# A hybrid decoder step in four groups: group barriers and the loop replaced by one straight program with semaphores that count on

## What is computed

```
xn = rms_norm(h, norm_mix)
qa, ka, va, qkv_b, z, a, b, gate_logits = split(xn @ w_in)
oa = sliding-window attention with sinks (qa, ka, va)
qb, kb, vb = silu(short_conv(qkv_b));  ob = gated delta rule(qb, kb, vb, a, b), gated norm with z
ga, gb = split(sigmoid(gate_logits))
h = h + (ga * (oa @ w_oa) + gb * (ob @ w_ob)) @ w_out
hn = rms_norm(h, norm_ffn)
h = h + (silu(hn @ w_gate) * (hn @ w_up)) @ w_down
y = rms_norm(h, norm_final)
```

## Time and profile before

| | us |
|---|---|
| median of 3 runs | 3794.16 (3791.37 to 3797.62) |
| the profiled execution | 3792.9 |
| its span, first to last instruction | 3791.1 |
| TensorE busy | 3594.3 (95%) |
| VectorE busy | 1808.2 (48%) |
| ScalarE busy | 1330.6 (35%) |
| GpSimd busy | 307.4 (8%) |

### The profile page before, as it was taken

One profiled execution on the slowest core, in us unless ns is written; L12 is line 12 of the kernel. 1 busy time (PEld: TensorE's weight loads), 2 busy tenths in 40 slices (PEclk: granted clock), 3 DMA queues, 4 the chain that ended last, 5 costly groups with the idle time before them and its releaser, 6 DMA issues. The chain is left out here.

```text
span 3791.1 us, 49730 instructions
## 1 busy us (share of the span) xinstructions
PE 3594.3 (95%) x20199; PEld 3103.6 (82%) x20199; DVE 1808.2 (48%) x3160; ACT 1330.6 (35%) x2360; POOL 307.4 (8%) x297
## 2 busy tenths in 40 slices
PE   6879999999998999999998999999998999999997
PEld 6768888999997888788877888788886888788886
DVE  3844332543434744454344744454344654455344
ACT  3532333322223544432223544432223543442222
POOL 2111110000001211000000311000000221100000
PEclk9978889999999999999999999999999999999998
DMA  4101001322232211233333211233323211133323
GB/s 161 45 30 41 29 28 43 111 84 84 84 133 89 72 35 34 73 113 99 95 128 110 73 34 34 67 111 100 95 99 122 89 40 34 59 109 100 95 95 131
DMA packets 89484, 303.98 MB, mean 80 GB/s; under 512 B 12384, under 2 KB 14384, under 8 KB 88336
## 3 DMA queue, kind: packets, MB, share of 16 engines
q1 hardware_dynamic: 89248, 300.68, 24.3%
HBM read 289.04 MB, written 12.62 MB: 80 GB/s over the span
## 5 line engine op out<-in xcount | busy, mean ns | idle before, releaser
L611 PE MATMUL bank<-hnT,wh 128*128 128x512 f32 (+1 forms) x3520 | 931.4, 352 | 0.0
L1519 DVE TENSOR_TENSOR wl<-raw,wh 128x1024 fp32r<-128x1024 f32 (+1 forms) x472 | 585.6, 1241 | 651.0 <-ACT wh L1161 648.7
L611 PE MATMUL bank<-xnT,wh 128*128 128x512 f32 (+2 forms) x2560 | 746.4, 378 | 12.4 <-DVE d_dT L1753 9.7
L611 PEld LDWEIGHTS bank<-hnT,wh 128*128 128x128 f32 x3520 | 619.4, 188 | 91.4 <-issue 0.2
L1161 ACT CAST wh<-raw 128x1024 fp32r<-128x1024 f32 (+1 forms) x472 | 492.3, 1043 | 435.7 <-PE bank L611 329.4
L611 PE MATMUL bank<-hnT,wl 128*128 128x512 f32 (+1 forms) x1760 | 622.2, 354 | 0.0
L611 PEld LDWEIGHTS bank<-xnT,wh 128*128 128x128 f32 x2560 | 454.5, 196 | 81.3 <-DVE d_dT L1753 11.0
L611 PE MATMUL bank<-hid,wh 128*128 128x512 f32 (+1 forms) x1760 | 468.6, 354 | 6.4 <-DVE wl L1519 5.1
L611 PE MATMUL bank<-xnT,wl 128*128 128x512 f32 (+2 forms) x1280 | 471.0, 368 | 0.0
L611 PEld LDWEIGHTS bank<-hnT,wl 128*128 128x128 f32 x1760 | 330.6, 188 | 45.8
L611 PEld LDWEIGHTS bank<-hid,wh 128*128 128x128 f32 x1760 | 309.3, 188 | 55.1 <-DVE wl L1519 8.1
(11 more groups left out here) (300 smaller groups left out, 4647.1 us busy)
## 6 DMA issues: line engine op xcount, KB each, us to landing
raw<-in_wstream SPq DMA_DIRECT2D x474, 512.0 KB, 3.4
xr<-in_x_prompt SPq DMA_DIRECT2D x20, 512.0 KB, 5.1
xT<-in_xT SPq DMA_DIRECT2D x5, 2048.0 KB, 11.9
hT<-in_xT SPq DMA_DIRECT2D x4, 2048.0 KB, 9.0
out_yp_out<-hT SPq DMA_DIRECT2D x16, 512.0 KB, 3.0
raw<-in_wstream SPq DMA_DIRECT2D x8, 528.0 KB, 3.4
Sb<-in_state_delta SPq DMA_DIRECT2D x1, 2048.0 KB, 12.4
out_ds_out<-Sb SPq DMA_DIRECT2D x1, 2048.0 KB, 6.4
```

The source lines that it names most:

```text
L611: ins = nc.tensor.matmul(*a, **k)
L1519: v_.tensor_tensor(wl[n % HL][:, 0:m], raw[:, n % RAW, 0:m], wh[n % HL][:, 0:m].bitcast(F32), ALU.subtract).then_inc(sem("lo_done"), 1)
```

## The change

All four groups are written out one after another, and each engine has one list from the prologue to the epilogue: one block in place of many, no barrier between groups, no loop, no clearing of semaphores.

- Since nothing sets a semaphore back, each wait that counts within a group now adds what earlier stages have counted: `made(name, v)` adds to v from a table COUNTS of what the prologue, group 0 and each later group add.
- The ring of weights runs on over the groups: unit numbers are g * NU + n. A group's last roundings on ACT and DVE already include the next group's first two units, by the same rule "two units ahead" that holds inside a group; `ahead_hi` and `ahead_lo` are gone.
- TensorE's claims on its eight banks go on over the join, and at each a1 unit it waits for two further chunks of the normed input.
- The scratch tokens' last norm stands in group 1, beside the last norm of group 0's prompt tokens (banks 5 and 6, semaphores with an S in their names). Their output is stored there.
- Group 3 no longer loads and norms a next group's input or rounds weights for it.
- ACT waits, ahead of the squares of each delta tile, for POOL's root of the tile before.

The diff, cut to its core (nearly every other line only moves to the left or wraps a wait in `made`):

```
+    now = [0]
+    def made(name, v):
+        pro, first, later = COUNTS.get(name, (0, 0, 0))
+        k = now[0]
+        return sem(name), v + (pro if k > 0 else 0) + (first if k > 1 else 0) + later * max(k - 2, 0)
...
-    def ahead_hi(act, n):
-        act.wait_ge(sem(f"ahead_in{n}"), 16)
-        act.copy(wh[n][:, 0:width(n)], raw[:, n, 0:width(n)]).then_inc(sem("ahead_hi"), 1)
-    def ahead_lo(dve, n):
-        dve.wait_ge(sem("ahead_hi"), n + 1)
...
+    def load_until(sp, n):
+        while asked[0] <= min(n, NG * NU - 1):
+            k = asked[0]
+            if k >= RAW:
+                sp.wait_ge(sem("lo_done"), k - RAW + 1)
+            m = width(k % NU)
+            sp.dma_start(raw[:, k % RAW, 0:m], d["wstream"][k % NU][:, 0:m]).then_inc(sem(f"raw_in{k % RAW}"), 16)
+            asked[0] += 1
...
             def unit(name, i):
-                    n = UNIT_AT[(name, i)]
-                    if n >= PRE:
-                        pe.wait_ge(sem("lo_done"), n - PRE + 1)
+                n = g * NU + UNIT_AT[(name, i)]
+                pe.wait_ge(sem("lo_done"), n + 1)
...
                         if u == 0:
                             claim(abank[t], "a_rd", q + 1)
+                        if q == 0:
+                            pe.wait_ge(*made("xl_done", 2 * u + 2 - KD))
...
                     if not first and u == 0:
                         claim(2, "ypre_done", 1)
+                        pe.wait_ge(*made("yacc_done", 0))
                         last_sums(pe, tiles, 2)
+                        if g == 1:
+                            claim(5, "ypreS_done", 1)
+                            last_sums(pe, ["S"], 5, "S")
...
-                if first:
-                    pe.wait_ge(sem("yacc_done"), KD - 1)
-                    claim(7, "ypre_done", 1)
-                    last_sums(pe, ["S"], 7)
-                    claim(4, "y_done", KD)
-                    last_spread(pe, ["S"], 4)
...
-                while split[0] <= min(UNIT_AT[(name, i)] + AHEAD, NU - 1):
+                while split[0] <= min(g * NU + UNIT_AT[(name, i)] + AHEAD, NG * NU - 1):
...
-                for n in range(PRE):
-                    dve.wait_ge(sem("unit_started"), NU - 1 + n)
-                    ahead_lo(dve, n)
...
-    prologue()
-    nc.all_engine_barrier(sems_to_clear=range(nums[0], nums[-1] + 1))
-    group(0, True)
-    nc.all_engine_barrier(sems_to_clear=range(nums[0], nums[-1] + 1))
-    with nc.Fori(1, NG) as g:
-        group(g, False)
-        nc.all_engine_barrier(sems_to_clear=range(nums[0], nums[-1] + 1))
-    epilogue()
+    stages = [prologue()] + [group(g, g == 0) for g in range(NG)] + [epilogue()]
+    with nc.Block() as block:
+        @block.tensor
+        def _(pe):
+            claim = make_claim(pe)
+            for stage in stages:
+                stage[1](pe, claim)
```

More of the change, by code:

```diff
@@ L336, in claim @@
                 pe.wait_ge(*released[b])
-            released[b] = (sem(s), v)
+            released[b] = made(s, v)
         return claim
-    def last_sums(pe, order, b):
-        row_sums(pe, order, b, acc, "ysum_ps")
-    def last_pre(dve, order, b):
-        n = n_of(order[0])
-        dve.wait_ge(sem("ysum_ps"), 1)
-        nc.vector.tensor_scalar(yr[0:n, 0:len(order)], bank[b][0:n, 0:len(order)], 1.0 / DM, EPS, ALU.mult,
-                                ALU.add).then_inc(sem("ypre_done"), 1)
@@ L358, in last_spread, with last_root @@
+    def last_root(pool, order, x=""):
+        n, q = n_of(order[0]), 0 if x == "" else NT
+        pool.wait_ge(*made(f"ypre{x}_done", 1))
+        nc.gpsimd.tensor_tensor(yr[0:n, q:q + len(order)], yr[0:n, q:q + len(order)], nhalf[0:n, 0:len(order)],
+                                ALU.pow).then_inc(sem(f"yrr{x}_done"), 1)
+    def last_spread(pe, order, b, x=""):
+        q0 = 0 if x == "" else NT
+        pe.wait_ge(*made(f"yrr{x}_done", 1))
         for q, t in enumerate(order):
-            last = spread(t, yr, q, bank[b][:, P * q:P * q + n_of(t)])
@@ new lines, in tensor, with scalar @@
+        def tensor(pe, claim):
+            now[0] = 0
+            pe.wait_ge(*made("ident_in", 16))
+            for q, t in enumerate(tiles):
+                pe.wait_ge(*made("rr_done", q + 1))
+                spread(t, rr, q, bank[5][:, 0:NS] if t == "S" else bank[6][:, P * t:P * (t + 1)]).then_inc(sem("xR_ps"), 1)
+            pe.wait_ge(*made("const_in", 16))
+        def scalar(act):
+            now[0] = 0
+            act.wait_ge(*made("param_in", 16))
+            act_steps[0] += 1
+            act.activation(nal[:], p("alog"), ACT.Exp).then_inc(sem("act_step"), 1)
+            for q, t in enumerate(tiles):
+                act.wait_ge(*made(f"x_in{t}", 32 if t == "S" else 16))
+                x_square(act, t, q, xr0[t])
+            for k in range(KD):
+                x_hi(act, k, xT0, every)
@@ new lines, in tensor, with scalar, gpsimd, vector @@
+        def tensor(pe, claim):
+            now[0] = 1 + NG
+            claim(2, "ypre_done", 1)
+            pe.wait_ge(*made("yacc_done", 0))
+            last_sums(pe, order, 2)
+            claim(7, "y_done", KD)
+            last_spread(pe, order, 7)
+        def scalar(act):
+            pass
+        def gpsimd(pool):
+            now[0] = 1 + NG
+            last_root(pool, order)
+        def vector(dve):
+            now[0] = 1 + NG
+            last_pre(dve, order, 2)
+            last_scale(dve, order, 7)
@@ L502, in group @@
+        return sync, tensor, scalar, gpsimd, vector
     def group(g, first):
@@ L1718, in _ @@
-                dve.wait_ge(sem("tail_done"), NCONV)
-                lo_until("conv", NCONV - 1)
-                quarters = [0]
-                def beside(t, k):
-                    for _ in range(0 if t == "S" else QUARTERS[k]):
-                        quarters[0] += 1
-                        if quarters[0] % 4 == 0:
-                            lo_until("gate", quarters[0] // 4 - 1)
-                    if after(t) is not None:
-                        attention_step(after(t), IN_DELTA_S if t == "S" else IN_DELTA, k)
```

2785 lines of the change are left out of this document (1431 added, 1354 removed).

## The result

The changed kernel takes 3724.01 us in the median of four runs (3722.45 to 3731.46), against 3792.76 (3789.59 to 3797.62) for the kernel before on the same chip. The ratio is 0.9822, with a 95% interval from 0.9804 to 0.9839. The forecast was 3735, with a range of its own from 3726 to 3746. The direction and the mechanism held. The kernel before was 1.4 us faster here than the 3794.16 that the forecast started from; 0.9822 of 3794.16 is 3726.6, at the range's edge. The profiled execution took 3722.45 us, 70.4 less in its span than the one before, where 58.7 had been worked out.

The account below looks back on a forecast made before the run. TensorE's work and its pauses were taken as the bound. Joins 46.2, start 2.6 and end 9.9 make 58.7 us off the profiled 3792.9: 3734.2, plus 1.3 for the median, forecast 3735; own range 3726 to 3746, given range to 3752.

Parts of the forecast that it names:

- What bounds the kernel: Whole kernel: TensorE, busy 3594.3 of 3791.1 us, plus the places where it stands still, the long ones at the joins.
- The joins: Three group joins, last matmul to first sum: 64.1 us become 17.2, less 0.7 for scratch tokens' steps; gain 46.2 us.
- All three covers: At the joins, TensorE's work hides VectorE's tail; thinnest, the first unit covers the `acc` sums by 0.3 us.
- the first rival: Joins close only in part, the first unit needing VectorE's tail: 16 to 22 us given back, 3751 to 3757; 12 in 100.
- The start: Group 0's start: TensorE waits for the first unit's low part alone, starting at about 30.05, not 32.69; gain 2.6 us.
- The end: Group 3's spreads and epilogue: 0.8 fewer spreads, 7.2 earlier sums, 1.9 full pace; gain 9.9 us, or 8.0 if pace fell.
- I take the full pace for both: Last sums and spreads in the epilogue: 0.95 and 1.05 us instead of 1.86 and 2.08; gain 1.9 us.
- Group 3: Group 3 prepares no next input, so TensorE loses 8 spreads; gain some 0.8 us.
- The delta stages: Delta stages: instructions and order unchanged; the granted clock may shift the time by 8 us either way.
- a sign of being wrong: Prediction wrong if the three joins give back over 10 us, or the delta stages change by more than that.
- The slower program on account of instruction fetches: Rival: the written-out program stalls on instructions; 42 stops of 3.6 us would cost 151 us, 3886; 2 in 100.
- the loop's head: Join at the loop's head: TensorE starts 3.6 us after SP, put down to the jump; already in the sum.

Follow-up runs that it names:

- The kernel with barriers: Changed kernel with each stage in its own block, a barrier of all engines between blocks and no loop: 3759.63 us, ratio 0.9916.
- the copy: The changed kernel run a second time, word for word: 3727.09 us, ratio 0.9829.
- The kernel with the loads alone: Changed kernel, but group 3 still loads a next input and does not norm it: 3730.08 us, ratio 0.9833.
- the one with the loads apart: Changed kernel with first two weight units rounded early, idle matmuls at start and end, and next-input loads spread between weights in SP's queue: 3710.86 us, ratio 0.9785.
- the kernel with early units: Changed kernel, but the prologue rounds the first two weight units after the second and fourth input chunk, not the eighth: 3720.75 us, ratio 0.9814.

## Why the prediction was right, and where it was off

**What bounds the kernel** held: TensorE's work and its pauses. Apart from the added matmuls, every difference that the traces could place was a pause of TensorE or went with its clock.

**The joins** came as forecast, 47.1 us for 46.2. All three covers held, the thinnest by 0.14 us. The kernel with barriers shows what would be left if only the loop had gone (35.6 us given back), and the one that waits for the whole input what the first rival would have cost: 20.3 us at the joins, inside the 16 to 22 that it was priced at, and 24.5 in all.

**The start** gave 2.2 for 2.6. VectorE's two low parts began later than the 28.78 of the earlier trace rows, and TensorE began 0.15 us behind the first of them, as forecast:

```profile
29.15 2.36 DVE L1615 TENSOR_TENSOR wl<-raw,wh 128x1024 fp32r<-128x1024 f32 x2 [0.20 <-ACT wh L1261]
```

The pause before it stayed, and 8 us of it could be had by casting earlier.

**The end** had one step that failed: "So I take the full pace for both: 1.9 us more." Only the sums had it in the profiled execution (1.02 us; the spreads 2.05), and in the copy neither had (1.84 and 2.05). The ground for the step was a pair of such matmuls at 0.32 us behind a pause of 5.24, and eight behind a shorter pause did not follow it every time. The term was 0.9 and can be 0. Without the 0.8 of group 3 the forecast for the end was 9.1, or 7.2 if the pace had fallen. Measured were 7.9, and 7.1 in the copy, so 7.2 was the better value. The Trainium skill (TensorE: Matmul & The Clock Gate, What's actually happening) says that the chip watches activity at moments that are not tied to the program, so one kernel measures differently from run to run. The two executions agree with that: 1.02 and 1.84 us behind the same 2.34 of pause. The rule of the Trainium skill (the same section) that the resting state is the throttled one, taken strictly, gives the 7.2, which the copy bears out and the profiled execution only for the spreads.

**Group 3** was the mis-sized term: "TensorE loses the 8 spreads at 3738.55, some 0.8 us". It lost 3.1, because with the preparation 4 MB of loads went too, and the weights' ring no longer ran dry: 1.6 us of waits went, and some 0.7 us that groups 1 and 2 lost as well. In the trace of before this stood in each of groups 1 to 3, where the second down half begins, as one wait for `wl` of 1.25 to 1.58 us and one of some 0.35 behind it. In group 1:

```profile
1984.44 0.73 PE L611 MATMUL bank<-hid,wh 128*128 128x512 f32 x2 [1.25 <-DVE wl L1519]
```

The forecast counted the instructions that went on TensorE, VectorE and ScalarE, and not SP's. The kernel with the loads alone puts 2.2 us of it back, and the one with the loads apart takes 1.5 and 1.7 from two other groups. That the loads cost this is shown, and that the same bytes cost TensorE no wait when they stand apart in the queue. How much of it is bandwidth and how much the place in the queue is not told apart.

**The delta stages** were taken as unchanged, with 8 us either way for the clock. They gave 9.0, just over the edge of that allowance, and this is most of the 11 us by which the forecast was high. With the faster first units the stretches changed by 13.9, past the 10 that the prediction had named as a sign of being wrong; without them they stayed under it. Over the twelve traces, 36 stretches in groups 1 to 3, I set their length from the first sums on against the time in it at the lower of TensorE's two levels. It follows 377.4 us and 0.36 for each us at that level (correlation 0.96). Before, that time is 51.3 us in the three stretches, after 27.2, and 24.1 by 0.36 is 8.7, close to the 9.0. (The allowance had reckoned with a half lost for each us, where 0.36 is measured.)

So the gain is real in this run, and it is not a fixed part of the change. In the eight other traces without a pause at every join that time is 27 to 48 us, and the same three stretches, from the first sums on, gain 1.0 to 7.6 us on the kernel before. The 9.0, counted alike, is the highest of the nine, and 3.0 stands in the middle. In particular the kernel with early units, whose order in these stages is the same, has 44.4 us and gains 2.2. Nor do the pauses at the joins set it: the two other kernels with a pause at each join had 34 and 44 us. What decides which stretches fall to the lower level stays open.

**The rivals.** The slower program on account of instruction fetches did not show: fewer packets, and TensorE's waits put down to "issue" inside groups are 3.7 us in both traces. For the loop's head the barrier kernel bears out the split: without a jump TensorE follows SP by 0.2 us and not 3.6.

## What to carry to other kernels

Price a join from the last matmul of one part to the first fixed point of the next, and split it into the slowest engine's tail, the barrier and the jump: here 7.7 with the two ahead casts (5.4 without), 2.0 with the clearing (0.6 for a plain barrier) and 3.6, together 13.3 us. The tail is hidden only if the next part's first work needs nothing from it. When a step goes, list its DMAs as well, and look for waits on whatever stood behind them in the queue, however short. Where small matmuls alternate with pauses, allow for the granted clock by what the same stage varies between executions, here 4 to 5 us in 390, and run the same kernel twice before a gain of that size is believed.

## What the runs showed of the hardware that was not expected

- The same kernel's stretch of 384 to 389 us moved from group to group between two executions, with a granted clock of 1.00 in the short one and 0.98 in the long ones.
- A us at the lower level went with 0.36 us more in the delta stage and not with a half (36 stretches of twelve traces). That other things than TensorE's pace bound part of it would explain this; it is not shown.
- Eight useless matmuls ahead of the first unit made it start at 0.23 us a matmul in place of 0.43; fillers ahead of the last spreads made them 1.13 us long in place of 2.05.
- A plain barrier over the engines cost 0.8 us behind the slowest engine. At the loop's head TensorE came 3.6 us after SP, at the plain barrier 0.2.
- 4 MB of input loads ahead of a ring of weights cost TensorE 1.5 to 2.2 us in a stretch where the DMA engines were busy for 0.32 of the time in the mean: a low mean share does not mean that a load comes in time.
